# A four-layer block on one core: constants, first panel and x land in parts, and three panels run on the unscaled residual before the vectors are turned

## What is computed

```
h = x
xn = rmsnorm(h, norm_g[i])          # h * rsqrt(mean(h*h) + 1e-6) * g
proj = xn @ w_in[i]                 # 1024 -> 4376 columns
(hq, hf, hi, hgo, hz, nq, ...) = split(proj)
```

## Time and profile before

| what | value |
|---|---|
| median of the runs | 1121.53 us (1120.48 to 1123.28, 3 runs) |
| the profiled execution, its own time | 1121.01 us |
| its span, first to last instruction | 1119.1 us |
| PE busy | 1054.6 us (94%) |
| DVE, ACT busy | 716.9 us (64%), 601.6 us (54%) |
| mean granted PE clock | 0.972 of 2.4 GHz |
| chain of work that ended last, by engine | PE 74%, DVE 11%, ACT 8%, issue 3%, DMA 3% |
| mean DMA rate | 146 GB/s |

### The profile page before, as it was taken

How to read it: one execution, slowest core, us unless ns; L and a number is a source line. 1 busy time by engine, 2 the same in 40 slices (tenths; PEclk the granted TensorE clock), 3 DMA queues, 4 the chain that set the end, 5 groups by cost and what they waited for, 6 DMA issues and landing times.

```text
span 1119.1 us, 21428 instructions
## 1 busy us (share of the span) xinstructions
PE 1054.6 (94%) x9017; PEld 994.2 (89%) x9017; DVE 716.9 (64%) x1080; ACT 601.6 (54%) x876; POOL 4.9 (0%) x13
## 2 busy tenths in 40 slices
PE   5999888999998988999999999999999899999997
PEld 5988767899996876999999999999979799999997
DVE  6746556567557356588858757667653558666574
ACT  5643565467435554477646555545645456445553
POOL 1000000000000000000000000000000000000000
PEclk9999899999999899999999999999989899999998
DMA  9543422254646221285543655556372235555531
GB/s 284 187 122 112 153 76 76 76 162 145 189 118 190 75 76 38 76 264 165 183 151 117 224 188 180 178 177 195 89 224 78 76 119 184 188 187 187 187 113 38
DMA packets 144748, 163.59 MB, mean 146 GB/s; under 512 B 6072, under 2 KB 135552, under 8 KB 144672
## 3 DMA queue, kind: packets, MB, share of 16 engines
q1 hardware_dynamic: 143752, 161.04, 44.8%
q10 hardware_dynamic: 632, 1.30, 0.3%
q0 software_dynamic: 288, 0.14, 0.1%
HBM read 161.43 MB, written 1.05 MB: 145 GB/s over the span
## 4 chain that ended last, share of the span: by engine, by line
PE 74%; DVE 11%; ACT 8%; issue 3%; DMA 3%; SPq 0%; ACTq 0%; DVEq 0%
PE ps L441 22%; PE ps L442 21%; PE ps L443 21%; DVE panels_low L1697 4%; ACT panels_high L1165 4%; DMA panels<-in_w_in 3%; ACT probs L1151 2%; PE ps L531 2%; PE ps L459 2%; DVE neg_max L1720 1%; DVE probs L1736 1%; PE ps L662 1%; PE ps L569 1%; PE ps L557 1%; DVE unscaled L1672 1%
## 5 line engine op out<-in xcount | busy, mean ns | idle before, releaser
L1697 DVE TENSOR_TENSOR panels_low<-panels,panels_high 128x2048 fp32r<-128x2048 f32 (+1 forms) x146 | 330.2, 2264 | 263.9 <-ACT panels_high L1165 263.7
L441 PE MATMUL ps<-input_high,panels_low 128*128 128x256 f32 x1600 | 464.7, 290 | 16.0 <-DVE input_low L1692 7.6
L442 PE MATMUL ps<-input_low,panels_high 128*128 128x256 f32 x1600 | 456.7, 285 | 0.0
L443 PE MATMUL ps<-input_high,panels_high 128*128 128x256 f32 x1600 | 456.5, 285 | 0.0
L1165 ACT CAST panels_high<-panels 128x2048 fp32r<-128x2048 f32 (+1 forms) x146 | 274.2, 1880 | 142.5 <-PE ps L443 119.2
L441 PEld LDWEIGHTS ps<-input_high,panels_low 128*128 128x128 f32 x1600 | 311.3, 195 | 22.3 <-issue 7.4
L442 PEld LDWEIGHTS ps<-input_low,panels_high 128*128 128x128 f32 x1600 | 311.4, 195 | 0.3
L443 PEld LDWEIGHTS ps<-input_high,panels_high 128*128 128x128 f32 x1600 | 311.0, 194 | 0.0
L441 PE MATMUL ps<-ffn_hidden_high,panels_low 128*128 128x256 f32 x352 | 99.2, 282 | 3.1 <-issue 2.9
L442 PE MATMUL ps<-ffn_hidden_low,panels_high 128*128 128x256 f32 x352 | 99.5, 283 | 0.0
L443 PE MATMUL ps<-ffn_hidden_high,panels_high 128*128 128x256 f32 x352 | 99.4, 282 | 0.0
(11 more groups left out here) (285 smaller groups left out, 1333.8 us busy)
## 6 DMA issues: line engine op xcount, KB each, us to landing
panels<-in_ffn_up SPq DMA_DIRECT2D x44, 1024.0 KB, 5.1
panels<-in_w_in SPq DMA_DIRECT2D x32, 1024.0 KB, 5.5
panels<-in_ffn_down SPq DMA_DIRECT2D x22, 1024.0 KB, 4.9
panels<-in_mix_w_in SPq DMA_DIRECT2D x20, 1024.0 KB, 5.5
panels<-in_w_out SPq DMA_DIRECT2D x8, 1024.0 KB, 5.2
panels<-in_w_pg SPq DMA_DIRECT2D x8, 1024.0 KB, 5.2
panels<-in_mix_w_out SPq DMA_DIRECT2D x8, 1024.0 KB, 5.5
panels<-in_w_pp SPq DMA_DIRECT2D x2, 1024.0 KB, 4.8
```

What stands on the lines that cost most here:

```text
L441: pe.matmul(dst, w[1], x[0], start=start, stop=False if not kw else True, **kw)
L442: pe.matmul(dst, w[0], x[1], start=False, stop=False if not kw else True, **kw)
L443: return pe.matmul(dst, w[0], x[0], start=False, stop=stop, **kw)
L1697: V.tensor_tensor(low_slots[slot][:, 0:size], raw[n % SLOTS][:, 0:size], high_slots[slot][:, 0:size].bitcast(F32), ALU.subtract).then_inc( ...
```

## The change

Transfers. The constants are loaded in two parts: identity and ones (the first 256 columns, 128 KB) first by ACT, the rest (about 564 KB) by SP behind panel 1. The first vector transfer (16 rows of `norm_g`, "factors") gets a semaphore of its own. The two halves of x get a semaphore each. The first panel (hf0) is loaded in two halves of four chunks each. The vectors' rows land in VH's memory instead of QN's.

PE. It starts with 8 products of a block of zeros with itself into a spare bank. It turns the factors, then x, tile by tile. The first panels are then hf0 alone (chunk by chunk, as the half panels and the operand get ready), hf1 with the sum of squares between its column halves, the vectors' transposes, and hq0 on the unscaled operand. hq1 is the first to use the normed operand.

ACT and DVE. ACT copies the factors and a quarter of x (DVE the other three), makes the unscaled high parts between the casts of the half panels, then casts hf1, squares, casts hq0, makes RINV and the normed high parts, copies the vectors, and only then waits for `dve_part`. DVE scales hf0, norms, scales hf1, scales hq0, makes two small bf16 constants, and then runs the lower-bound chain.

```diff
-            pe.wait_ge(x_landed, 32)
-            for g in range(4):
-                begin(f"x{g}", g)
-                for j in range(4):
-                    c, n = 2 * g + j // 2, j % 2
-                    ins = pe.transpose(ps[g][:, j * P:(j + 1) * P], xt[:, n, c * P:(c + 1) * P], ident)
-                done(f"x{g}", ins)
+            pe.wait_ge(zeros_ready, 1)
+            for i in range(8):
+                pe.matmul(ps[7][:, 0:P], ZR[:, :], ZR[:, :], start=True, stop=True)
+            pe.wait_ge(const_landed, 16)
+            pe.wait_ge(factors_landed, 16)
+            begin("factors", 4)
+            done("factors", pe.transpose(ps[4][:, 0:16], vrows[0:16, 0, :], ident[0:16, 0:16]))
+            for n in range(NT):
+                pe.wait_ge(x_landed if n == 0 else x_second_landed, 16)
+                for g in range(4):
+                    if n == 0:
+                        begin(f"x{g}", g)
+                    for i in range(2):
+                        c = 2 * g + i
+                        ins = pe.transpose(ps[g][:, (2 * i + n) * P:(2 * i + n + 1) * P],
+                                           xt[:, n, c * P:(c + 1) * P], ident)
...
+            def unscaled_panel(key, b, sum_too=False):
...
+                        ins = product3(ps[b][:, j * T:(j + 1) * T], [t[:, k, j * P:(j + 1) * P] for t in parts(key)],
+                                       (uh[k], ul[k]), k == 0, k == ND - 1)
+                    if j == 0 and sum_too:
+                        norm_sum(0)
...
+            def first_panels():
...
+                for k in range(ND):
+                    if k == 0:
+                        pe.wait_ge(half_low_ready, 1)
+                    if k == ND // 2:
+                        split(key)
+                    pe.wait_ge(u_ready, k + 1)
...
+                unscaled_panel(("hf1", 0), 2, sum_too=True)
+                by_pool = len(vec_dmas[2::3])
+                pe.wait_ge(const_rest_landed, 16)
+                pe.wait_ge(vec_landed, 16 * (N_VEC_DMAS - by_pool - 1))
+                pe.wait_ge(pool_vec_landed, 16 * by_pool)
+                for g in range((NVT + 3) // 4):
...
+                unscaled_panel(("hq0", 0), 3)
...
+                for g in range(2) if l > 0 else (1,):
+                    two_chunks(f"hq{g}_{l}", 3 + g, (f"hq{g}", l), normed=nidx if g == 0 or l == 0 else None)
```

On ACT, from the copy of the factors on:

```diff
+            log_exp()
             act.wait_ge(eps_ready, 1)
-            squares(0, lambda g: drained(act, f"x{g}"))
+            copy_out("factors", VC[:, 0:16], bank("factors")[:, 0:16])
+            copy_out("x3", H[:, 3 * 512:4 * 512], bank("x3")[:, :])
+            drained(act, "factors")
+            drained(act, "x0")
+            unscaled_high(0, 0)
+            half = PANEL // 2
+            act.wait_ge(half_panel_landed, 16)
+            nc.scalar.copy(high_slots[0][:, 0:half], raw[0][:, 0:half]).then_inc(half_high_ready, 1)
+            drained(act, "x1")
+            unscaled_high(0, 1)
+            act.wait_ge(panel_landed[0], 16)
+            nc.scalar.copy(high_slots[0][:, half:PANEL], raw[0][:, half:PANEL]).then_inc(high_ready, 1)
...
+            for g in (2, 3):
+                drained(act, f"x{g}")
+                unscaled_high(0, g)
             split_high(-1, 2)
...
             for g in range(4):
-                unscaled_high(0, g)
+                f(sq3[:, 2 * g:2 * g + 2, :], h3[:, 2 * g:2 * g + 2, :], ACT.Square).then_inc(sq_ready, 1)
             split_high(-1)
             norm(0)
+            for g in range((NVT + 3) // 4):
+                n0, n1 = 16 if g == 0 else 512 * g, min(512 * (g + 1), NVEC)
+                copy_out(f"vec{g}", VC[:, n0:n1], bank(f"vec{g}")[:, n0 - 512 * g:n1 - 512 * g])
             act.wait_ge(dve_part, 1)
             f(SPC[:, 8:20], SPC[:, 8:20], ACT.Exp).then_inc(act_part, 1)
```

On DVE, behind the low parts of the first three panels:

```diff
+            split_low(-1)
+            dve.wait_ge(rinv_ready, 1)
+            scale_out("hf0_0", FG[:, 0:512])
+            normed(0, "norm_g", 0)
+            scale_out("hf1_0", FG[:, 512:1024])
+            scale_out("hq0_0", QP[:, 0:512])
+            dve.wait_ge(const_rest_landed, 16)
             V.tensor_copy(IDB[:, :], ident)
             step(V.tensor_copy(NGB[:, :], const("causal_neg")))
...
             for g in range((NVT + 3) // 4):
                 drained(dve, f"vec{g}")
-            for g in range(4):
-                unscaled_low(0, g)
-            split_low(-1)
-            normed(0, "norm_g", 0)
+            settle()
```

On the SP queue:

```diff
+            sp.dma_start(xt[:, 0, :], xsrc[:, 0, :]).then_inc(x_landed, 16)
+            sp.dma_start(xt[:, 1, :], xsrc[:, 1, :]).then_inc(x_second_landed, 16)
...
+            sp.dma_start(panel[:, 0:ND // 2, :], wsrc[:, 0:ND // 2, :]).then_inc(half_panel_landed, 16)
+            sp.dma_start(panel[:, ND // 2:ND, :], wsrc[:, ND // 2:ND, :]).then_inc(panel_landed[0], 16)
             load_panel(1)
+            sp.dma_start(CN[:, 2 * P:NCONST], a["const_table"][:, 2 * P:NCONST]).then_inc(const_rest_landed, 16)
```

More of the change, by code:

```diff
@@ L605, in output @@
                         norm_sum(nidx, b, (g - 1,))
[L607 to L616, removed]
+            def unscaled_panel(key, b, sum_too=False):
+                name = f"{key[0]}_{key[1]}"
+                begin(name, b)
+                for j in range(2):
+                    for k in range(ND):
+                        if j == 0 and k == 0:
+                            split(key)
[3 more added lines that the diff above has]
+                        norm_sum(0)
+                done(name, ins)
+                release(key)
@@ new lines, in first_panels @@
+            def first_panels():
+                key = ("hf0", 0)
+                begin("hf0_0", 1)
+                for k in range(ND):
+                    if k == 0:
+                        pe.wait_ge(half_low_ready, 1)
+                    if k == ND // 2:
+                        split(key)
+                    pe.wait_ge(u_ready, k + 1)
+                    for j in range(2):
+                        ins = product3(ps[1][:, j * T:(j + 1) * T], [t[:, k, j * P:(j + 1) * P] for t in parts(key)],
+                                       (uh[k], ul[k]), k == 0 and j == 0, True, skip_group_check=True)
+                done("hf0_0", ins)
+                release(key)
+                unscaled_panel(("hf1", 0), 2, sum_too=True)
[4 more added lines that the diff above has]
+                for g in range((NVT + 3) // 4):
+                    begin(f"vec{g}", 6 + g)
+                    for j in range(min(4, NVT - 4 * g)):
+                        r = min(P, NVEC - (4 * g + j) * P)
+                        ins = pe.transpose(ps[6 + g][:, j * P:j * P + r], vrows[0:r, 4 * g + j, :], ident[0:r, 0:r])
+                    done(f"vec{g}", ins)
+                unscaled_panel(("hq0", 0), 3)
@@ L627, in _ @@
                     norm_sum(nidx, 0, (0, 1))
[L628 to L631, removed]
+                    first_two([f"hf{g}_{l}" for g in range(2)], (1, 2), [(f"hf{g}", l) for g in range(2)], nidx,
+                              0, {3: (2,), 6: (3,)})
+                else:
+                    first_panels()
+                for g in range(2) if l > 0 else (1,):
+                    two_chunks(f"hq{g}_{l}", 3 + g, (f"hq{g}", l), normed=nidx if g == 0 or l == 0 else None)
                 tokens([f"hi{n}_{l}" for n in range(NT)], 5, [(f"hi{h}", l) for h in range(2)])
@@ L1208, in squares @@
             def squares(nidx, ready, between=None, quarters=range(4)):
-                if 3 in quarters and (nidx == 0 or nidx not in gains):
+                if 3 in quarters and nidx not in gains:
                     log_exp()
@@ L1213, in squares @@
                     ready(g)
-                    if nidx > 0 and nidx in gains:
+                    if nidx in gains:
                         unscaled_high(nidx, g)
@@ L1218, in squares @@
                         between(g)
-                if 3 in quarters and nidx > 0 and nidx in gains:
+                if 3 in quarters and nidx in gains:
                     log_exp()
@@ L1296, in _ @@
                 for g in range(2):
[L1297 removed]
+                    if (g, l) != (0, 0):
+                        copy_out(f"hq{g}_{l}", QP[:, g * 512:(g + 1) * 512], bank(f"hq{g}_{l}")[:, :])
                     split_after(f"hq{g}_{l}")
@@ L1750, in add_out @@
                         unscaled_low(nidx, g)
+            V.memset(ZR[:, :], 0.0).then_inc(zeros_ready, 1)
             V.memset(EPSC[:, 0:1], EPS)
             V.memset(EPSC[:, 1:2], 1.0).then_inc(eps_ready, 1)
-            for t in (AD, AB, KZ, KCZ):
+            for t in (AD, AB, KZ):
                 V.memset(t[:, :], 0.0)
-            step(V.memset(ZR[:, :], 0.0))
-            dve.wait_ge(const_landed, 16)
+            step(V.memset(KCZ[:, :], 0.0))
+            for g in range(3):
+                full(dve, f"x{g}")
+                V.tensor_copy(H[:, g * 512:(g + 1) * 512], bank(f"x{g}")[:, :]).then_inc(free(f"x{g}"), 1)
+            drained(dve, "x2")
```

(24 more changed lines are left out.)

24 lines of the change are left out of this document (14 added, 10 removed).

## The result

The changed kernel takes 1126.41 us (median of 5 runs, 1125.6 to 1128.56), the kernel before 1121.53 on the same chip. The ratio of the times is 1.005, with a 95% interval of 1.0036 to 1.0063. By the medians the change costs 4.9 us, by the interval 4 to 7 us. The profiled execution took 1128.56 us with a span of 1126.8, so it lies 2.2 us above its own median.

A forecast was written before the change was run, and what follows sets the result against it. PE was taken as the bound, busy 1054.6 of 1119.1 us. hq1 starting 2.8 us later plus 2.4 us of slow clock gave +5.2, from 1121.53 to 1126.7 us; range 1121 to 1130, leaving out the second rival.

The forecast's parts named there:

- hf0's first product: PE at the front: with x and half panels landing earlier, hf0 starts at 12.6 us instead of 20.9.
- sum of squares inside hf1: PE in hf1: 16 passes formerly in idle time now lie on the path, 3.5 us.
- PE idle ahead of hq1: PE between hq0 and hq1: waits for hq1's low part, 6.3 us (6.0 to 6.5).
- loss to the slow stretch behind it: PE in hq1: lower clock after the idling for 3.4 to 6.3 us, losing 1.7 to 3.2, taken as 2.4.
- The main step: Ahead of hq1: its cast waits for dve_part, signalled only after hq0's scaling; PE idles 6.3 us, hq1 starts 2.8 us later.
- hf0's slow stretch: PE in hf0: lower clock expected after idling from 8.6 to 12.6 us, costing 1.7 to 2.7 us.
- The first (a better front): Front: hf0 at full clock, hf1 starts at 19.0, later stretch costs 1.7; change +3.1, 1124.6 us; chance 0.20.
- The second (no wait): Ahead of hq1: its cast is made before hq0 ends, no slow stretch follows; 1118.0 us; chance 0.10.
- The third (the halves are no earlier): Front transfers: x's second tile and first half land no earlier than 8.4 and 13.3 us; 1129.7 us; chance 0.15.
- eight transposes: PE ahead of hf0: behind x's second tile at 6.8 us, 0.228 us each, 1.8 us.
- the shift at hq1: hq1's start and end: work behind is unchanged, so its shift, +5.2 us, is the change of the whole time.

The follow-up runs named there:

- the order mended: Changed kernel with vectors turned between hf0 and hf1, and hq1's cast, hi0's cast and the lower-bound chain moved earlier; 1119.51 us, ratio 0.9977.
- the best version: Changed kernel with the order mended, eight more zero products ahead of hf0, and the lower-bound chain and Exp ahead of hq1's cast; 1117.23 us, ratio 0.9955.

## Why the prediction was right

It gave 1126.7 us; 1126.41 was measured. By its steps, in the profile of the changed kernel:

| step | predicted | profile |
|---|---|---|
| second half panel landed | 11.7 us | 2.13 + 8.8 = 10.9 |
| panel 1 landed | 14.5 | 3.12 + 11.4 = 14.5 |
| hf0's first product | 12.6 | 13.13 |
| hf1's low part ready | 19.0 | 16.95 + 2.29 = 19.2 |
| hf0 ended | 20.4 | 20.9 |
| sum of squares inside hf1 | 3.5 | 3.46 |
| hq0 ended | 36.3 | 36.7 |
| PE idle ahead of hq1 | 6.3 | 6.17 |
| hq1's first product | 42.6 | 42.88 |
| loss to the slow stretch behind it | 2.4 | 2.3 |
| hq1's products out, against before | +5.2 | +5.4 |

The last line is ACT's copy of hq1. The two rows are those of the kernel before and of the changed kernel:

```profile
45.72 0.59 ACT L1156 COPY query<-ps 128x512 f32<-128x512 f32 x1 [2.75 <-PE ps L443]
51.15 0.59 ACT L1204 COPY query<-ps 128x512 f32<-128x512 f32 x1 [3.67 <-PE ps L447]
```

**The main step** was to read the wait out of the order on two engines: a cast behind an Exp, the Exp behind a DVE chain, the chain behind the scaling of the last unscaled panel. It is shown from both sides: alone it costs 7.4 us in the old kernel, and with the order mended the new front is 2.4 us faster than the old (ratio 0.9977).

**What the front gained** was given back in two parts, as the prediction had it. hf0 starts 7.8 us earlier, but the sum of squares and the vectors' transposes (4.3 us) now stand between panels, where PE did them in idle time before, and hf0's slow stretch costs some 0.3 us more than the one in the old kernel. That left 3.1 us at hq0's end (hq1 could have started at 36.7 instead of 39.76), and the 6.2 us wait with its slow stretch of 2.3 us took these and 5.4 us more.

**Rivals.** The first (a better front) isn't what the medians show (1126.41 and 1127.44 us against 1124.6), yet a second profile of the same kernel looks like it in part, below. The second (no wait) is out for the change as written. The third (the halves are no earlier) is out by the landing times: x's second tile landed at 1.20 + 5.1 = 6.3 us and the first half panel at 1.66 + 7.4 = 9.0, not at 8.4 and 13.3.

**What was mis-sized.** Three terms of the front were off by a little. The prediction let eight transposes run behind the landing of x's second tile; PE turned all sixteen in one go from 5.74 us on, so their rate set the end, not the landing, and hf0 started 0.5 us later than predicted. A slow stretch was priced at half its length; by the spacing of the products it costs 0.44 of it (0.213 against 0.120 us). And the slow stretch in hf0 was put down to PE's idling before it. In the profile the zeros and the transposes ahead of that idling were slow already, so idling isn't shown to be the reason there.

The rate of the transposes, taken as 0.228 us each, isn't fixed either. In the second profile of the changed kernel all 16 took 2.0 us instead of 3.7, hf0 started at 11.60 instead of 13.13, and hq1's products were out 3.9 us later than in the kernel before, instead of 5.4. The rows, of the changed kernel's first and second profile (count, busy us, mean ns; by line and form):

```profile
L558 PE MATMUL ps<-consts,forget_key 128*128 128x128 f32 x16 | 3.7, 424 | 0.0
```

```profile
L558 PE MATMUL ps<-consts,forget_key 128*128 128x128 f32 x16 | 2.0, 276 | 0.0
```

**Where the agreement is luck.** The prediction took the shift at hq1 for the shift of the whole time. In the profile it was 5.4 us at hq1 and 7.7 us at the end of the span (1126.8 against 1119.1). 1.0 us came at one later wait, and 1.5 us near 890 us, where the clock stayed low for longer. The rows, first of the kernel before, then of the changed kernel, the wait and then the stretch (columns as in the earlier trace rows):

```profile
359.42 0.39 PE L537 MATMUL ps<-cmp_hidden,cmp_w 128*128 128x32 f32 x1 [2.68 <-issue]
365.99 0.39 PE L541 MATMUL ps<-cmp_hidden,cmp_w 128*128 128x32 f32 x1 [3.68 <-issue]
```

```profile
883.00:893.00 10.00, 8.46 (x60) 7.98 (x57) 4.38 (x8) 2.23 (x4) 0.00 (x0) 0.74 0.06 21
889.40:899.40 10.00, 8.46 (x47) 7.98 (x44) 3.98 (x7) 2.23 (x4) 0.00 (x0) 0.58 0.06 20
```

Neither is a fixed cost of the change: with its front, the later wait is 2.5 us in the profile without the zeros at the start, and near 890 us the second profile has 0.74 like the kernel before. In the second profile the shift went from 3.9 us at hq1 to 4.7 at the end (1123.8). In the kernel with the wait alone it went from 8.5 to 6.9. In the best version, with its zeros, a gain of 4.9 us at hq1 was 2.4 at the end. So a shift at the front reached the end to within some 2.5 us. The direction and the rough size of the forecast follow from its mechanism; that the median came within 0.3 us of the sum is luck in part. Why the later wait is about 2.6 us in some profiles and 3.7 in others stays open.

## What to carry to other kernels

When work is moved ahead, read what the moved step now stands in front of on its own engine: here a scaling of 0.7 us that waits for the last early panel was put ahead of the chain on which the next panel's cast hangs, and a stall of 6.2 us came of it. Idle time of a helper engine is where such a chain belongs, in front of the transfer that it would wait for anyway. Count such a stall of PE with the slow stretch behind it: in the seven profiles with the wait of 6.2 us, the first 16 to 28 products behind it were slow, which cost 1.5 to 2.6 us on top. Don't expect a change of a few us at the front to reach the end of a long program to the tenth.

## What the runs showed of the hardware that I had not expected

The clock at the front differs between executions of one kernel. The changed kernel turned x at 0.23 us a transpose in one profile and at 0.125 in another; with more zeros, all of hf0's products were fast in one profile, and in another 15 of them were slow (12.1 to 15.3 us). The Trainium skill (TensorE: Matmul & The Clock Gate, What's actually happening) says that the same kernel can meet the clock gate at another phase at its start; the two profiles agree with that. What the zeros at the start do to the time can't be told from nothing (ratios 1.0034 without, 1.005 and 1.0047 with them).
